# A two-layer mixer-and-expert network: the second layer's modulation vectors computed in pieces inside the first layer's expert loop, and the first block written out without its layer loop

## The chip, the cores and the metric

The kernel runs on one core of one Trainium2 chip. The metric is the device time of one launch in microseconds. The kernel before took 3701.41 us, median of three runs (3700.87 to 3701.83). All arithmetic is float32. Where full precision in a matrix product is wanted, each operand is split into an upper part, rounded to the fp32r type, and the remainder, and three products of the parts are added.

## The reference, cut to what matters

Two blocks follow each other, both two layers deep, on 256 tokens of width 1024. Only the first block is touched.

```python
cond = silu(c)                                   # c is (1, 1024): one vector for all tokens
for l in range(2):
    mod = cond @ ada_w[l] + ada_b[l]             # (1, 6144): six vectors of 1024
    sh1, sc1, g1, sh2, sc2, g2 = split(mod, 6)
    h = rms_norm(x, norm1_g[l]) * (1.0 + sc1) + sh1
    proj = h @ w_in[l]                           # then an SSD mixer, MoBA and sliding-window attention
    x = x + g1 * (concat(y_ssd, y_moba, y_swa) @ w_out[l])
    h = rms_norm(x, norm2_g[l]) * (1.0 + sc2) + sh2
    x = x + g2 * peer_ffn(h, ...)                # 8 heads x 16 of 16384 one-neuron experts
x = rms_norm(x, final_g)
# second block, unchanged: feed-forward, hybrid mixer, memory attention, feed-forward, twice
```

The modulation `mod` depends on `c` and the weights alone, not on `x`, in both layers. `ada_w[l]` is 1024 x 6144 floats, 24 MB. `peer_ffn` is computed densely: all 16384 experts are applied to all tokens, and a sparse matrix of gates picks the chosen ones.

## The kernel before, in words

Each engine has a program of its own; they meet at semaphores. The first block stands in a loop over the two layers (`Fori(0, DEPTH)`) on every engine. A layer has four stages.

1. The modulation stage. SyncE loads `ada_w[l]` in twelve tiles of 2 MB into the four slots of `weights` (L537). Of each tile's eight chunks of 128 rows VectorE multiplies and sums six (L1556, L1559), TensorE takes two (L763), adds the bias (L768) and sums VectorE's part over the partitions with a matrix of ones (L770), and ScalarE copies the row, which then stands on all partitions, to `mod` (L1147). After the fourth tile VectorE also normalizes `x` and `mem` (L1463, L1528, L1551). The end is `modulated` (L1534, L1538), which writes `h`, and TensorE transposes `mem` and `h` (L641).
2. The mixers, from the product with `w_in` (L718, L725, L685, L691) to the one with `w_out`, and then the queries and keys of the experts.
3. The choice of the experts on VectorE, beside the first layer of the experts' products.
4. The expert loops. The expert weights come in 256 parts of 1 MB for each layer of the network (here called steps; `expert_order` numbers them 0 to 127 per layer of the network). SyncE loads a part into one of four raw buffers. ScalarE makes its upper part (L1164), VectorE the lower (L1495; GpSimd, L622, for the first 22), TensorE multiplies: a step of the experts' first layer is L685 and L691 (`first_layer`), a step of the second is L923 (`second_layer`). TensorE goes through steps 0 to 19, then 20 to 35 with two groups of gates after each (L902; VectorE makes their one-hot tiles, L1825 and L1826), then 36 to 39; from step 40 on 12 rounds of two first-layer and two second-layer steps, and at last, in steps 88 to 127, second-layer steps alone. After each second-layer step VectorE waits for its end, gates the hidden values of one later step (L1842, L1843, L1845), and then makes a lower part two steps ahead. TensorE starts its accumulator banks with four products with zeros (L894) ahead of step 20, and closes them with L944. VectorE then multiplies by `g2` (L1870) and adds to `x` (L1874).

In this lace of rounds the order of every engine is fixed by the code; nothing is planned at run time. SyncE's queue carries all weight parts, the gates written to DRAM and read back (`scr<-gates`, 1 MB for every eight steps of the second layer), in the order of the code; ScalarE's queue carries the small parameter rows. Buffers on loan in stage 4: `mod` from column 2048 on and `rowp` hold activations of the experts (`gact`), so that `mod` holds only its first two vectors and the last one during the loops.

At the layer's end the loop branches back on all engines, and the modulation stage of the next layer begins. Its weights can be loaded as soon as the last expert parts have left the slots. Behind the second layer stands no modulation stage, but the final norm: there ScalarE takes the sum of squares (L1136) and a root (L1142), and VectorE a reciprocal (L1881) and one scaling (L1883).

## Time and profile before

| | |
|---|---|
| three runs | 3700.87 to 3701.83 us, median 3701.41 |
| the profiled execution | 3700.87 us, span 3699.1 us |
| TensorE busy | 3409.8 us (92%), mean granted clock 0.956 |
| VectorE, ScalarE, GpSimd busy | 2390.0, 1468.9, 229.0 us |
| first block, layer 0 | modulation 0 to about 89 us, experts' rounds and tail to 1099 us |
| first block, layer 1 | modulation 1099 to 1186 us, end at 2192 us |
| second block | 2192 to 3699 us |

The span runs from the first to the last instruction, and 1.8 us lie around it. A stage in which TensorE is busy throughout, with no wait recorded, is one whose length is TensorE's work; anything that another engine does there costs nothing as long as it is in time. A stage in which TensorE waits is one in which a chain through other engines sets the length.

### The profile page before, as it was taken

The numbers are of one execution on the slowest core, as the hardware profiler recorded it, in microseconds if no ns is written. First come the engines' busy times: TensorE is split into PE (matmuls) and PEld (weight loads), VectorE is DVE, ScalarE is ACT, GpSimd is POOL, SyncE is SP. The second block draws the span as 40 slices with busy tenths as digits, with TensorE's granted clock in tenths as the row PEclk, the third lists the DMA queues.
The fourth block names the chain that finished last, engine by engine and source line by source line (L and its number), as shares of the span: only waits on it lengthen the run. The fifth ranks groups of instructions, "written<-read, shape, count | busy, mean of one in ns | idle before, by whom it ended". The sixth has DMA issues, their size and how long they took to land.

```text
span 3699.1 us, 58720 instructions
## 1 busy us (share of the span) xinstructions
PE 3409.8 (92%) x22220; PEld 3087.8 (83%) x22220; DVE 2390.0 (65%) x4104; ACT 1468.9 (40%) x1545; POOL 229.0 (6%) x48
## 2 busy tenths in 40 slices
PE   6879999999997989999999989996989899978898
PEld 2879899998873879899998879896889798867897
DVE  6757996556768658996557765464545455546454
ACT  1434454333321434454343333444443343444433
POOL 0005600000000007500000000000000000000000
PEclk9989999999998989999999999997999999979999
DMA  9414467666767324466666765542335455423353
GB/s 367 171 69 160 157 222 251 207 211 225 245 215 316 137 103 161 163 223 239 213 214 228 246 233 191 182 171 80 138 140 184 168 179 195 158 102 123 142 183 137
DMA packets 154052, 688.78 MB, mean 186 GB/s; under 512 B 10339, under 2 KB 76771, under 8 KB 78947
## 3 DMA queue, kind: packets, MB, share of 16 engines
q1 hardware_dynamic: 149264, 663.79, 50.4%
q10 hardware_dynamic: 4564, 22.21, 1.6%
q8 instruction: 116, 1.90, 0.2%
q14 instruction: 108, 0.88, 0.1%
HBM read 649.26 MB, written 36.70 MB: 185 GB/s over the span
## 4 chain that ended last, share of the span: by engine, by line
PE 81%; DVE 10%; ACT 3%; issue 2%; DVEq 1%; DMA 1%; PEld 1%; ACTq 0%; PEldq 0%
PE ps L685 25%; PE ps L923 19%; PE ps L691 13%; PE ps L718 9%; PE ps L725 4%; PE ps L902 3%; DMA work<-in_mem 1%; ACT work L1156 1%; PE ps L763 1%; PE ps L657 1%; DVE position_hot L1802 1%; DVE position_hot L1805 1%; DVE scr L1767 1%; DVE scr L1760 1%; PE ps L770 1%
## 5 line engine op out<-in xcount | busy, mean ns | idle before, releaser
L1164 ACT ACTIVATE weights_upper<-weights 128x2048 fp32r<-128x2048 f32 x520 | 996.1, 1917 | 1694.4 <-PE ps L685 950.3
L1495 DVE TENSOR_TENSOR weights_lower<-weights,weights_upper 128x2048 fp32r<-128x2048 f32 x476 | 1090.3, 2291 | 749.1 <-ACT weights_upper L1164 748.3
L685 PE MATMUL ps<-hT_upper,weights_upper 128*128 128x256 f32 x4416 | 626.1, 284 | 3.5 <-ACT hT_upper L1326 3.5
L685 PE MATMUL ps<-hT_lower,weights_upper 128*128 128x256 f32 x4416 | 625.0, 284 | 0.2
L691 PE MATMUL ps<-hT_upper,weights_lower 128*128 128x256 f32 x4416 | 575.3, 283 | 4.1 <-POOL weights_lower L622 4.1
L685 PEld LDWEIGHTS ps<-hT_upper,weights_upper 128*128 128x128 f32 x4416 | 571.9, 192 | 7.1 <-ACT hT_upper L1326 6.7
L685 PEld LDWEIGHTS ps<-hT_lower,weights_upper 128*128 128x128 f32 x4416 | 571.1, 192 | 4.6 <-issue 1.0
L691 PEld LDWEIGHTS ps<-hT_upper,weights_lower 128*128 128x128 f32 x4416 | 549.7, 192 | 5.0 <-POOL weights_lower L622 5.0
L622 POOL TENSOR_TENSOR weights_lower<-weights,weights_upper 128x2048 fp32r<-128x2048 f32 x44 | 228.8, 5214 | 1299.3 <-ACT weights_upper L1164 1299.3
L923 PE MATMUL ps<-weights_upper,hidden_lower 128*128 128x512 f32 x1024 | 253.5, 390 | 0.0
L923 PE MATMUL ps<-weights_upper,hidden_upper 128*128 128x512 f32 x1024 | 252.9, 389 | 0.0
L923 PE MATMUL ps<-weights_lower,hidden_upper 128*128 128x512 f32 x1024 | 252.9, 389 | 0.0
L923 PEld LDWEIGHTS ps<-weights_lower,hidden_upper 128*128 128x128 f32 x1024 | 192.2, 188 | 39.9
L923 PEld LDWEIGHTS ps<-weights_upper,hidden_upper 128*128 128x128 f32 x1024 | 192.2, 188 | 39.9
L923 PEld LDWEIGHTS ps<-weights_upper,hidden_lower 128*128 128x128 f32 x1024 | 190.8, 188 | 38.5
L1826 DVE TENSOR_SCALAR scr<-cst,scr 128x128 f32<-128x128 f32 x512 | 187.7, 367 | 0.0
L1825 DVE TENSOR_SCALAR scr<-cst,scr 128x128 f32<-128x128 f32 x512 | 160.2, 313 | 0.2
L1842 DVE TENSOR_TENSOR hidden_upper<-work,scr 128x512 fp32r<-128x512 f32 x80 | 55.4, 693 | 119.3 <-PE ps L923 119.3
L902 PE MATMUL ps<-scr 128*128 128x128 f32 x1024 | 121.4, 277 | 0.0
L902 PEld LDWEIGHTS ps<-scr 128*128 128x128 f32 x1024 | 119.1, 191 | 0.0
L657 PE MATMUL ps<-diag,x_res 128*128 128x128 f32 x256 | 43.9, 351 | 59.6 <-DVE diag L1906 59.6
L718 PE MATMUL ps<-weights_upper,hT_lower 128*128 128x512 f32 (+2 forms) x352 | 91.6, 383 | 5.2 <-DVE hT_lower L1508 5.2
(311 smaller groups left out, 3478.7 us busy)
## 6 DMA issues: line engine op xcount, KB each, us to landing
weights<-in_parts SPq DMA_DIRECT2D x264, 1024.0 KB, 4.8
weights<-in_experts SPq DMA_DIRECT2D x256, 1024.0 KB, 4.8
weights<-in_ada_w SPq DMA_DIRECT2D x24, 2048.0 KB, 11.3
scr<-gates SPq DMA_DIRECT2D x32, 1024.0 KB, 8.1
gates<-h SPq DMA_DIRECT2D x16, 1024.0 KB, 4.8
gates<-work SPq DMA_DIRECT2D x16, 1024.0 KB, 4.8
mod<-in_row ACTq DMA_DIRECT2D x3, 1536.0 KB, 6.2
rowp<-in_row ACTq DMA_DIRECT2D x2, 1550.0 KB, 19.6
```

Source lines behind the costliest of these rows:

```text
L622: g.tensor_tensor(lower[:, p_.r % SPLIT, :], raw[:, p_.r, :], upper[:, p_.r % SPLIT, :].bitcast(F32), ALU.subtract).then_inc(lower_ready, 1)
L657: m = mm(k.bank(name, i)[:, (2 * e + t) * P:(2 * e + t + 1) * P], x[:, t, c * P:(c + 1) * P], diag[:, t, :], start=True, stop=True, skip_g ...
L685: m = mm(bank[:, e * T:(e + 1) * T], up[:, c, e * P:(e + 1) * P], s_[:, c, :], start=(e == 0 and n == 0 and c == 0), stop=False, skip_grou ...
L691: m = mm(bank[:, e * T:(e + 1) * T], lo[:, c, e * P:(e + 1) * P], src[0][:, c, :], start=False, stop=(c == KC - 1), skip_group_check=True)
L718: m = mm(k.bank(name, fill + t)[:, 0:cols], s_[:, c, t * P:(t + 1) * P], up[:, c - 4 * i, 0:cols], start=(n == 0 and c == 0), stop=False, ...
L725: m = mm(k.bank(name, fill + t)[:, 0:cols], src[0][:, c, t * P:(t + 1) * P], lo[:, c - 4 * i, 0:cols], start=False, stop=(c == chunks - 1) ...
L902: m = mm(k.bank("G", j)[:, t * P:(t + 1) * P], hotA[:, i_buf, 4 * j + t, :], hotB[:, i_buf, 4 * j + t, :], start=True, stop=True, skip_gro ...
L923: m = mm(k.bank("acc", 2 * t_ + dh), src[:, u, c, t_ * P:(t_ + 1) * P], w[:, c, dh * NBLK:(dh + 1) * NBLK], start=False, stop=False, skip_ ...
L1164: f(upper[:, p_.r % SPLIT, :], raw[:, p_.r, :], ACT.Copy).then_inc(upper_ready, 1)
L1495: v.tensor_tensor(lower[:, s, :], raw[:, p_.r, :], upper[:, s, :].bitcast(F32), ALU.subtract)\
L1825: v.tensor_scalar(hotA[:, i % 2, j, :], iota, ET[:, 0, t:t + 1], None, ALU.is_equal)
L1826: m = v.tensor_scalar(hotB[:, i % 2, j, :], iota, ET[:, 1, t:t + 1], ET[:, 2, t:t + 1], ALU.is_equal, ALU.mult)
```

## The change

Layer 0's modulation stage stays. For layer 1 the stage is gone. In its place:

- The weights `ada_w[1]` come as 96 pieces of 128 x 512 floats, 256 KB each (`ada_s`), eight for each of twelve stretches of 512 columns. SyncE loads them between the expert parts of layer 0 into four buffers in `work` (`load_ada`).
- VectorE adds each piece, times its value of `cond`, to an accumulator in `scr` (`ada_piece`, L1986). `ada_sub_step` gives the step: six pieces in each of the 12 rounds (two in the first step, two in the second, one in the third, one in the fourth), and one in each of the steps 88 to 111.
- Two steps after a stretch's last piece TensorE sums it over the partitions with one column of ones (`ada_rows`, L946), a product of one row by 512 columns; ScalarE copies that row out in two halves (L1369); SyncE writes them to DRAM (`keep_row`, 1 KB each). Twelve times each.
- ScalarE's queue reads the vectors back onto all partitions (`mod_back`), in three transfers at steps 88 and 112 and after the layer, and loads layer 1's `rowp` at step 118. At step 122 VectorE makes `(1 + sc1) * norm1_g` (L2017).
- At the layer's end ScalarE takes squares and roots as for the final norm, and VectorE makes `h` with `scaled_and_shifted` (a reciprocal, L1688, L1691). The first two parts of `w_in[1]` have their upper and lower parts made in steps 126 and 127.
- The first block is written out on all engines, TensorE's rounds too; the waits there compare with constants. The products with zeros moved from ahead of step 20 to after step 39, on both layers.

```diff
+def ada_sub_step(s):
+    turn, i = divmod(s, 6)
+    if turn < TURNS - AHEAD:
+        return 2 * AHEAD + 4 * turn + (0, 0, 1, 1, 2, 3)[i]
+    return 2 * AHEAD + 4 * (TURNS - AHEAD) + s - 6 * (TURNS - AHEAD)
...
@@ SyncE @@
+                def load_ada(s):
+                    tile = s // KC
+                    if s % KC == 0:
+                        if tile:
+                            sp.wait_ge(S("ada_used"), s - 7)
+                        else:
+                            sp.wait_ge(S("bias_zero"), 1)
+                        sp.dma_start(ada_bias_row[0:1, :], a["ada_b"][1:2, tile * NBLK:(tile + 1) * NBLK])\
+                            .then_inc(S("ada_bias_in"), 16)
+                    if s >= 4:
+                        sp.wait_ge(S("ada_used"), s - 3)
+                    sp.dma_start(ada_sub(s), a["ada_s"][s]).then_inc(ada_landed[s % 4], 16)
+                def keep_row(tile):
+                    sp.wait_ge(*k.emptied("row", 0, tile))
+                    for b in range(2):
+                        c = tile * NBLK + b * (NBLK // 2)
+                        sp.dma_start(ada_dram[0:1, c:c + NBLK // 2], ada_row[b]).then_inc(ada_kept[b], 16)
                 for n, (layer, t, u) in enumerate(expert_order()):
                     e = expert_part(l, 0, n)
                     sp.wait_ge(*e.raw_free())
+                    sp.dma_start(raw[:, e.r, :], a["experts"][l, n]).then_inc(raw_landed[e.r], 16)
+                    if l + 1 < DEPTH:
+                        for s in range(ADA_SUBS):
+                            if ada_sub_step(s) + 4 == n:
+                                load_ada(s)
...
+                            if ada_sub_step(KC * tile + KC - 1) + 10 == n:
+                                keep_row(tile)
...
@@ TensorE @@
-            with pe.Fori(0, DEPTH) as l:
+            for l in range(DEPTH):
...
-                for i in range(12):
+                for i in range(0 if l else 12):
...
+                def ada_rows(n):
+                    for tile in range(ADA_TILES if l + 1 < DEPTH else 0):
+                        if ada_sub_step(KC * tile + KC - 1) + 2 == n:
+                            pe.wait_ge(*k.free("row", 0, tile))
+                            pe.wait_ge(S("ada_used"), KC * tile + KC)
+                            mm(k.bank("row")[0:1, :], ones[:, 0:1], ada_acc[tile % 2], start=True, stop=True,
+                               skip_group_check=True).then_inc(k.fill_sem("row"), 1)
...
-                with pe.Fori(0, TURNS - AHEAD) as it:
-                    for u in range(2):
-                        first_layer(it, 2 * AHEAD + u, it + AHEAD, u)
-                    for u in range(2):
-                        second_layer(it, 2 * AHEAD + 2 + u, it, u)
...
+                for n in range(2 * AHEAD, EXPERTS):
+                    layer, t, u = order[n]
+                    (first_layer, second_layer)[layer](n, t, u)
+                    ada_rows(n)
...
@@ ScalarE, in the loop over the steps n @@
+                    elif l + 1 < DEPTH:
+                        upper_part(part(firsts[l + 1], 0, "win", n + SPLIT - EXPERTS))
+                    if l + 1 < DEPTH:
+                        for tile in range(ADA_TILES):
+                            if ada_sub_step(KC * tile + KC - 1) + 3 == n:
+                                ada_take(tile)
+                        if n == 2 * AHEAD + 4 * (TURNS - AHEAD):
+                            mod_back(0, 2)
+                        if n == 112:
+                            act.wait_ge(S("gated"), 2 * (AHEAD + 3))
+                            mod_back(2, 5)
+                        if n == 118:
+                            act.wait_ge(S("gated"), 2 * (AHEAD + 6))
+                            row1_in(1)
...
+                    for t in range(TT):
+                        act.wait_ge(S("x_peer"), l * TT + (t + 1))
+                        square_sum(x[:, t, :], h[:, t, :], t)
+                        deviation(t, t, EPS1_COL)
...
@@ VectorE @@
+                def ada_piece(s):
+                    tile, i = divmod(s, KC)
+                    acc = ada_acc[tile % 2]
+                    if i == 0:
+                        if tile >= 2:
+                            v.wait_ge(*k.filled("row", 0, tile - 2))
+                        v.wait_ge(S("ada_bias_in"), 16 * tile + 16)
+                        v.sem_inc(S("held"), 1)
+                    v.wait_ge(ada_landed[s % 4], 16 * (s // 4) + 16)
+                    v.drain()
+                    v.scalar_tensor_tensor(out=acc, in0=ada_sub(s), scalar=cT[:, i:i + 1],
+                                           in1=acc if i else ada_bias_row, op0=ALU.mult, op1=ALU.add)\
+                        .then_inc(S("ada_used"), 1)
...
                     if n + SPLIT < EXPERTS:
                         lower_part(expert_part(l, 0, n + SPLIT))
+                    elif l + 1 < DEPTH:
+                        lower_part(part(firsts[l + 1], 0, "win", n + SPLIT - EXPERTS))
...
+                    scaled_and_shifted(mod[:, D:2 * D], mod[:, 0:D], TT, "h1")
```

On VectorE, in a round before, the two first-layer steps and the first of the two second-layer steps; L1495 makes a lower part, L1842 to L1845 gate hidden values, and the rows between compute what a wait compares with:

```order
L1495 TENSOR_TENSOR weights_lower<-weights,weights_upper 128x2048
L1493 REGISTER_ALU
L1495 TENSOR_TENSOR weights_lower<-weights,weights_upper 128x2048
L1855 REGISTER_ALU
L1834 REGISTER_ALU
L1842 TENSOR_TENSOR hidden_upper<-rowp,scr 128x512
L1843 TENSOR_TENSOR rowp<-rowp,scr 128x512
L1845 TENSOR_TENSOR hidden_lower<-rowp,hidden_upper 128x512
L1493 ISA
L1495 TENSOR_TENSOR weights_lower<-weights,weights_upper 128x2048
```

And in the changed kernel, layer 0, the same steps, from behind the first lower part; L1613 is the lower part, L1969 to L1972 the gating, L1986 the pieces:

```order
L1986 SCALAR_TENSOR_TENSOR scr<-work,stats,scr 128x512 x2
L1613 TENSOR_TENSOR weights_lower<-weights,weights_upper 128x2048
L1986 SCALAR_TENSOR_TENSOR scr<-work,stats,scr 128x512 x2
L1969 TENSOR_TENSOR hidden_upper<-mod,scr 128x512
L1970 TENSOR_TENSOR mod<-mod,scr 128x512
L1972 TENSOR_TENSOR hidden_lower<-mod,hidden_upper 128x512
L1613 TENSOR_TENSOR weights_lower<-weights,weights_upper 128x2048
L1986 SCALAR_TENSOR_TENSOR scr<-work,stats,scr 128x512
```

A piece always stands behind the lower part of its step, so it delays the gating of the next step and not the lower part of its own.

On TensorE, at the seam of the two layers before: the last second-layer step, the closing of the accumulators, and then, by way of the branch to the loop's head at L754, the modulation stage:

```order
L923 MATMUL ps<-weights_upper,hidden_upper 128x512 x8
L932 REGISTER_ALU
L923 MATMUL ps<-weights_lower,hidden_upper 128x512 x8
L940 REGISTER_ALU
L940 COMPARE_AND_BRANCH
L944 MATMUL ps<-cst 128x2 x4
L754 REGISTER_ALU
L754 COMPARE_AND_BRANCH
```

In the changed kernel the same place; L699 transposes `h` of layer 1, L776 is the product with the first part of `w_in`:

```order
L989 MATMUL ps<-weights_upper,hidden_upper 128x512 x8
L989 MATMUL ps<-weights_lower,hidden_upper 128x512 x8
L1006 MATMUL ps<-cst 128x2 x4
L699 MATMUL ps<-cst,h 128x128 x16
L776 MATMUL ps<-weights_upper,hT_upper 128x512 x4
L776 MATMUL ps<-weights_upper,hT_lower 128x512 x4
```

All of the modulation stage and the transposes of `mem` are gone from between them, and no branch is left.

On VectorE at the same seam, the changed kernel; L2028 and L2032 add the experts' output to `x`, L1626 makes the lower part of the transposed `h`:

```order
L1972 TENSOR_TENSOR hidden_lower<-work,hidden_upper 128x512
L1613 TENSOR_TENSOR weights_lower<-weights,weights_upper 128x2048 x3
L2028 TENSOR_TENSOR scr<-ps,mod 128x512 x2
L2032 TENSOR_TENSOR x_res<-x_res,scr 128x1024
L2028 TENSOR_TENSOR scr<-ps,mod 128x512 x2
L2032 TENSOR_TENSOR x_res<-x_res,scr 128x1024
L1686 RECIPROCAL stats<-stats 128x1
L1688 SCALAR_TENSOR_TENSOR h<-x_res,stats,mod 128x1024
L1691 TENSOR_TENSOR h<-h,mod 128x1024
```

Of the three lower parts two are new there, those of `w_in`; before they stood behind the modulation stage.

## Rows read from the trace of the kernel before

**Rows 1.** Busy time by stage: us, PE, PEld, DVE, ACT, POOL busy (instructions), clock, DMA share, GB/s.

```profile
871.00:1100.00 229.00, 229.00 (x1016) 189.75 (x1014) 170.01 (x162) 77.53 (x42) 0.00 (x0) 1.00 0.66 222
1100.00:1186.00 86.00, 59.46 (x124) 20.01 (x124) 68.79 (x100) 14.82 (x21) 0.00 (x0) 0.84 0.86 351
```

**Rows 2.** Timeline, layer 0 to layer 1: start us, us, engine, line, instruction, [idle before].

```profile
1099.50 0.95 PE L944 MATMUL ps<-cst 128*128 128x2 f32 x8
1099.82 1.29 DVE L1870 TENSOR_TENSOR scr<-ps,mod 128x512 f32<-128x512 f32 x2 [6.73 <-PE ps L944]
...
1110.90 0.08 DVE L1523 MEMSET work<- 128x24 f32 x1 [5.96 <-issue]
...
1183.66 2.36 DVE L1538 TENSOR_TENSOR h<-h,mod 128x1024 f32<-128x1024 f32 x2
...
1187.86 1.83 PE L718 MATMUL ps<-weights_upper,hT_upper 128*128 128x512 f32 x4
...
1192.28 1.82 PE L718 MATMUL ps<-weights_upper,hT_lower 128*128 128x512 f32 x4 [2.59 <-DVE hT_lower L1508]
...
1198.59 1.07 PE L718 MATMUL ps<-weights_upper,hT_upper 128*128 128x512 f32 x4
```

**Rows 3.** Timeline, layer 1 to the second block.

```profile
2191.69 0.95 PE L944 MATMUL ps<-cst 128*128 128x2 f32 x8
...
2197.15 0.29 ACT L1142 ACTIVATE stats<-stats 128x1 f32<-128x1 f32 x1
...
2197.79 1.28 DVE L1883 SCALAR_TENSOR_TENSOR x_res<-x_res,stats,scr 128x1024 f32<-128x1024 f32 x1
```

**Rows 4.** Timeline of TensorE in the rounds of the experts.

```profile
624.37 2.00 PE L923 MATMUL ps<-weights_upper,hidden_lower 128*128 128x512 f32 x8
...
635.28 1.12 PE L685 MATMUL ps<-hT_lower,weights_upper 128*128 128x256 f32 x8
...
646.79 2.00 PE L923 MATMUL ps<-weights_upper,hidden_lower 128*128 128x512 f32 x8
```

**Rows 5.** Timeline of VectorE in one of these rounds.

```profile
635.48 0.69 DVE L1842 TENSOR_TENSOR hidden_upper<-mod,scr 128x512 fp32r<-128x512 f32 x1 [0.73 <-PE ps L923]
...
637.46 2.29 DVE L1495 TENSOR_TENSOR weights_lower<-weights,weights_upper 128x2048 fp32r<-128x2048 f32 x1
```

**Rows 6.** Timeline, modulation stage: five sums, a product, and two weight loads.

```profile
1160.33 4.05 DVE L1559 SCALAR_TENSOR_TENSOR mod<-weights,stats,mod 128x512 f32<-128x512 f32 x5
...
1161.79 1.13 PE L770 MATMUL ps<-mod,cst 128*128 128x512 f32 x2
...
1163.79 0.19 PEld L763 LDWEIGHTS ps<-weights,stats 128*128 128x128 f32 x1 [0.24 <-issue]
...
1164.22 0.19 PEld L763 LDWEIGHTS ps<-weights,stats 128*128 128x128 f32 x1 [0.24 <-issue]
```

**Rows 7.** Timeline where the gate groups begin and end.

```profile
434.12 5.79 PE L894 MATMUL ps<-cst 128*128 128x512 f32 x8 [0.36 <-DVE scr L1475]
...
464.88 2.29 DVE L1495 TENSOR_TENSOR weights_lower<-weights,weights_upper 128x2048 fp32r<-128x2048 f32 x1
474.33 2.29 DVE L1495 TENSOR_TENSOR weights_lower<-weights,weights_upper 128x2048 fp32r<-128x2048 f32 x1
...
576.82 3.79 PE L902 MATMUL ps<-scr 128*128 128x128 f32 x32
...
586.20 3.79 PE L902 MATMUL ps<-scr 128*128 128x128 f32 x32
```

**Rows 8.** DMA issues in 871 to 1090 us: KB each, median us to landing.

```profile
weights<-in_experts SPq DMA_DIRECT2D x37, 1024.0 KB, 4.9
scr<-gates SPq DMA_DIRECT2D x9, 1024.0 KB, 8.2
```

**Rows 9.** DMA issues in 1100 to 1180 us.

```profile
rowp<-in_row ACTq DMA_DIRECT2D x1, 1550.0 KB, 13.8
colp<-in_col ACTq DMA_DIRECT2D x1, 148.0 KB, 15.3
```

315 lines of the change are left out of this document (188 added, 127 removed).

## The prediction

> **What bounds the kernel now.** I read the table of stages first, to see where TensorE has no idle time, then the list of TensorE's waits, then the order of time at the two seams of the first block. In 871 to 1100 us, layer 0's last expert steps, TensorE is busy for all 229 us at the full clock, while VectorE works 170 of them and the DMA engines are busy for 0.66 of the time [rows 1]. TensorE alone sets the length there: what another engine gets on top is free as long as it stays in time, and every product added on TensorE is paid. The modulation stage of layer 1 behind it is the opposite. In its 86 us TensorE has 59 us of work, much of it at half speed (the granted clock is 0.84 on average), and VectorE is the busier one with 69 us [rows 1]. The stage's weights come at 351 GB/s [rows 1]. The change takes this stage away, and puts its sums under a stage in which VectorE has room.
>
> **The seam.** I measure from the products that close the accumulators to the start of the second part of `w_in`: 1198.59 - 1099.50 = 99.1 us before [rows 2]. After the change nothing of the modulation is left there, and the nearest measured thing is the seam between layer 1 and the second block, where the same square sums and roots are made [rows 3]. Step by step from the closing products:
>
> - Two lower parts of `w_in` now stand ahead of VectorE's addition to `x`. The last one waits for TensorE's last product, so it starts where L1870 started, 0.32 us after the closing products began [rows 2], and takes 2.29 us [rows 5]: 2.3 us of delay.
> - From the closing products to the end of the first token half's root: 2197.44 - 2191.69 = 5.75 us [rows 3].
> - Then VectorE: a reciprocal (0.35 us to the start of the next), a scaling of 1.28 us [rows 3], an addition of 1.18 us (2.36 for two) [rows 2], some 0.1 us between: 2.9 us for each half, and the halves follow each other. 5.8 us.
> - From the last `h` to TensorE's first product with `w_in`: 1187.86 - 1186.02 = 1.8 us (1186.02 is 1183.66 + 2.36) [rows 2]. This holds the transposes and ScalarE's first copy.
> - The first four products take 1.83 us, the rest of the first part 1198.59 - 1192.28 = 6.3 us [rows 2]. The wait of 2.59 us between them [rows 2] was for VectorE, busy with the same two lower parts that are now made before; it goes. What is late next is the chain of ScalarE's copy and VectorE's subtraction, which fits in the 1.83 us.
>
> Sum: 2.3 + 5.75 + 5.8 + 1.8 + 1.8 + 6.3 = 23.8 us, where there were 99.1. **The seam gives 75.3 us.** The bounds are 70 (VectorE's and ScalarE's small waits a half longer) and 79 us (no delay by the lower parts, shorter halves).
>
> Part of these 99.1 us was the loop's own: VectorE's first instruction of layer 1 comes at 1110.90 with 5.96 us of idle that nothing recorded released [rows 2], behind its branch back. The Trainium skill (Runtime: NRT & Kernel Launch, section Instruction fetch mechanics) says that a taken branch out of the current pages waits for a fetch of code. The row agrees; by that rule the straight code has no such pause, and were it there still, the seam would give 6 us less.
>
> **Products added on TensorE.** Twelve sums over partitions, one each of 512 columns in plain float32. Such a product is two passes in the trace, and in a run of them the passes start 1164.22 - 1163.79 = 0.43 us apart [rows 6], 0.86 us each; one alone shows 1.13 us to its modelled end [rows 6]. Between the other products it costs its passes, with the next one's load beside it. 12 x 0.86 = 10.3, at most 12 x 1.13 = 13.6. I take 10.7 us. Nothing hides them, since TensorE has no idle time there.
>
> **Pieces added on VectorE.** 96 sums of 128 x 512. Five in a row with the drains took 4.05 us [rows 6], 0.81 us each, 78 us in all. A round takes TensorE 646.79 - 624.37 = 22.42 us, and a second-layer step half of 635.28 - 624.37, 5.45 us [rows 4]. In such a step VectorE starts the gating, 1.98 us later the lower part, and is done after 2.29 more [rows 5]: 4.27, with a piece 5.08 us of 5.45. In a first-layer step a lower part and two pieces are 3.9 us of (22.42 - 10.91) / 2 = 5.76. So every step closes in itself, and a gated value, needed one step after the end that VectorE waits for, has 5.45 - 0.6 - 1.98 = 2.9 us in hand. The pieces are hidden: 0 us. If the cover is gone, the waiting order is gating, lower part, TensorE. The far ends are 0 and 78 us (all on the path). The nearest row, VectorE in its rounds, speaks for 0, and I keep +4 for the 24 tight steps.
>
> **Transfers.** Six pieces a round are 1.6 MB. At 0.66 busy [rows 1] the DMA engines work 14.8 us of a round; at the 351 GB/s and 0.86 of the modulation stage [rows 1] the pieces take 1.6 / 0.351 x 0.86 = 3.9 us more, 0.83 of the round. An expert part lands in 4.9 us, a block of gates in 8.2 [rows 8], and a part is asked for about three steps ahead of its use, 15 us. The pieces are asked for two steps ahead, 11 us. Small transfers in the crowded stage landed in up to 15.3 us, though behind large ones [rows 9]. I take 0 us, with +8 as the other end. `rowp` has four steps and 5 us, about 27 us, to land before VectorE waits for it at step 122, with gating queued behind it; it took 13.8 [rows 9].
>
> The Trainium skill (DMA: Bandwidth & Descriptors, section Bandwidth) speaks against the cut: its rule is transfers of 1 MiB or more for three quarters of the peak, and these are 256 KB. Were their cost twice mine by that rule, an estimate, the DMA engines would be busy for 22.6 of 22.4 us, and the rounds would just become theirs.
>
> **Zeros moved.** The four products with zeros stood right behind a pause of TensorE and took 5.79 us to their modelled end [rows 7], part of it at 1.2 GHz, since at the other level four products are 4 x 0.86 = 3.4 us. That is what they take after step 39. Step 20 now meets the low clock and loses the 2.4 us of difference. But the gate groups are tied to VectorE too: its lower parts there come 9.45 us apart, with no idle, and TensorE's groups 9.38 us apart [rows 7]. So TensorE gains little by starting early and then pays the 3.4 us: I take +1 us a layer, 2 us, between -4 and +7.
>
> **Constants in the waits.** The register arithmetic ahead of waits goes on both layers, and so do the branches of the rounds. The rounds follow without a gap (10.91 + 2 x 5.76 is the 22.42 seen) [rows 4], so there is nothing to win in them. In the mixers I take -2 us in all, between 0 and -12.
>
> **Sum.** -75.3 + 10.7 + 0 + 0 + 2 - 2 = -64.6 us. The profiled execution took 3699.1 + 1.8 = 3700.9 us, 0.5 below the median of the runs. 3700.9 - 64.6 = 3636.3, and with the median's 0.5: **3637 us**. The bounds above give 3618 to 3662.
>
> **Rivals.**
>
> *VectorE comes late.* A piece costs more than its 0.81 us once its reading stands beside incoming transfers, or the waits between add up. At 1.3 us a second-layer step needs 5.6 us of 5.45, which costs 24 x 0.15 = 4 us in the tail; at 2.2 us, nearly three times the measured one, TensorE waits 1.0 us in each, which costs 25. For it speaks the thin margin of 0.37 us a step, against it that these sums ran at 0.81 us under the kernel's highest DMA rate [rows 1, 6]. Time: 3637 + 25 = 3662.
>
> *The transfers bind the rounds.* With the pieces at twice the price, plus gates, each of the 12 rounds and the 24 tail steps waits about 1 us: 36 us, 3673. Against it is the idle 0.34 of the DMA engines.
>
> *TensorE starves for code* (the slower side). The rounds ran from a short body held in a loop; now each step's 96 or so instructions and more are streamed, next to weights at 0.8 of the DMA engines. The place is every step of both layers, 256 in all, and it decides from 64.6 / 256 = 0.25 us a step. At 0.4 us it would be 102 us: 3739. Against it: VectorE's and ScalarE's code for these steps was straight already, and TensorE's code in the mixers is straight and runs without gaps.
>
> *More is saved.* If the pauses of the small stages were mostly register arithmetic and the mixers give 12 us: 3625.
>
> *Nothing happens*, the stage being replaced by another wait of the same length, say for the vectors read back from DRAM: these are asked for at steps 88 and 112, 40 and 16 steps of 5.45 us ahead of use. I give it 1 in 100.
>
> **How the numbers follow.** Forecast 0.72; VectorE late 0.10; transfers 0.05; more saved 0.09; code 0.03; nothing 0.01. The range is 3620 to 3665: it holds the forecast's bounds and most of the rivals on both sides. A measurement tells 0.2% (7 us) from no change. Faster 0.95, same 0.02, slower 0.03, as only the last two cases leave that side.
>
> **What would show it.** Between the closing products and the second part of `w_in` about 24 us; the twelve products one by one at 0.86 us distance added; no wait of TensorE in steps 40 to 127, with a round of layer 0 at 22.42 or 23.3 us; VectorE's pieces at 0.75 us busy; DMA busy about 0.8; layer 1 from there on as long as before, within 5 us. Waits of TensorE for lower parts, hidden parts or `weights_upper` in layer 0's rounds would make it wrong, as would idle time of TensorE between its own instructions.

## The result, and the profile after

The changed kernel took 3641.87 us, median of four runs (3641.30 to 3643.28), beside 3701.62 us (3700.87 to 3702.02) for the kernel before on the same chip: a ratio of 0.984, 95% interval 0.9829 to 0.9852. That is 59.8 us less, where 64.6 were forecast, and inside the range. The profiled execution has a span of 3640.6 us against 3699.1, with the same mean granted clock of 0.956.

First the stages. TensorE's first instruction of each marks its start, and the columns are microseconds.

| stage | before | after | difference | forecast |
|---|---|---|---|---|
| start to the experts chosen, layer 0 | 432.23 | 432.24 | 0 | 0 |
| gate groups to step 42, layer 0 | 192.14 | 194.27 | +2.13 | +1 |
| rounds and tail, layer 0 | 475.13 | 489.09 | +13.96 | +10.7 |
| the seam | 99.09 | 22.79 | -76.30 | -75.3 |
| mixers and choice, layer 1 | 325.75 | 324.97 | -0.78 | -2 |
| gate groups to step 42, layer 1 | 192.22 | 193.98 | +1.76 | +1 |
| rounds and tail, layer 1 | 475.13 | 475.13 | 0 | 0 |
| second block | 1507.4 | 1508.1 | +0.7 | 0 |

The sum is -58.5 us, the difference of the spans (3640.6 - 3699.1). The forecast's large term held; the row products are 3.3 us above it, and the gate stages, the mixers and the second block 1.9, 1.2 and 0.7 us.

Busy time by stage in the changed kernel, in the columns of [rows 1]; the second stretch is the seam:

```profile
871.00:1100.00 229.00, 229.00 (x1044) 187.72 (x1044) 191.84 (x190) 82.30 (x53) 0.00 (x0) 1.00 0.82 282
1116.00:1138.00 22.00, 11.13 (x44) 9.29 (x45) 14.89 (x18) 8.81 (x14) 0.00 (x0) 0.61 0.23 89
```

In the same 229 us as in [rows 1] VectorE works 191.8 us instead of 170.0 and the DMA engines are busy for 0.82 instead of 0.66, but TensorE has still no idle time and the full clock. The seam has 22 us where there were 99 us.

Most of that window lies in the tail, with one piece a step. The rounds, with six pieces each, before and then after:

```profile
655.00:871.00 216.00, 216.00 (x1406) 198.51 (x1405) 124.96 (x96) 84.23 (x58) 0.00 (x0) 1.00 0.62 212
655.00:885.00 230.00, 230.00 (x1444) 203.33 (x1443) 172.83 (x158) 89.75 (x75) 0.00 (x0) 1.00 0.78 271
```

The timeline of the seam, which answers to [rows 2]:

```profile
1115.60 0.95 PE L1006 MATMUL ps<-cst 128*128 128x2 f32 x8
1115.98 2.29 DVE L1613 TENSOR_TENSOR weights_lower<-weights,weights_upper 128x2048 fp32r<-128x2048 f32 x1 [3.15 <-ACT weights_upper L1226]
1118.19 1.28 DVE L2028 TENSOR_TENSOR scr<-ps,mod 128x512 f32<-128x512 f32 x2
...
1123.33 0.29 ACT L1204 ACTIVATE stats<-stats 128x1 f32<-128x1 f32 x1
...
1123.89 1.28 DVE L1688 SCALAR_TENSOR_TENSOR h<-x_res,stats,mod 128x1024 f32<-128x1024 f32 x1
...
1126.62 1.94 PE L699 MATMUL ps<-cst,h 128*128 128x128 f32 x8 [10.08 <-DVE h L1691]
...
1127.98 1.23 DVE L1691 TENSOR_TENSOR h<-h,mod 128x1024 f32<-128x1024 f32 x1
...
1130.95 2.06 PE L776 MATMUL ps<-weights_upper,hT_upper 128*128 128x512 f32 x4
...
1138.39 1.07 PE L776 MATMUL ps<-weights_upper,hT_upper 128*128 128x512 f32 x4
```

The reader finds each step of the forecast's chain. The lower part of `w_in` puts VectorE's first multiplication off to 1118.19, 2.59 us behind the closing products (forecast 2.3 behind the 0.32 us of before). The first root ends 8.02 us behind them (8.05 forecast), the last `h` 13.61 (13.85), TensorE's first product with `w_in` follows 1.74 us later (1.8), and the first part takes 7.44 us (8.1). TensorE's pause of 10.08 us waits for `h`. The pause at the loop's branch is gone. One link came out in number only: the profile puts the start of that lower part down to ScalarE's upper part, which is made from 1114.03 to 1115.95, and not to TensorE's last product, as the forecast had it. TensorE's last product ends at 1115.76, within 0.2 us of it, so the 2.3 us were met partly by luck.

In the rounds, TensorE around one of the twelve row products (L946), and PEld's rows for the loads there:

```profile
652.59 1.97 PE L989 MATMUL ps<-weights_lower,hidden_upper 128*128 128x512 f32 x8
654.49 1.02 PE L946 MATMUL ps<-scr,cst 128*1 128x512 f32 x2
655.44 2.11 PE L989 MATMUL ps<-weights_upper,hidden_lower 128*128 128x512 f32 x8
```
```profile
654.49 0.09 PEld L946 LDWEIGHTS ps<-scr,cst 128*1 128x1 f32 x2 [0.35 <-issue]
655.44 1.69 PEld L989 LDWEIGHTS ps<-weights_upper,hidden_lower 128*128 128x128 f32 x8 [0.86 <-ACT weights_upper L1226]
```

A group of eight products takes 1.815 us from start to start. From 652.59 to the group behind the next one, at 657.39, there are 4.80 us with the row product in between, so it costs 4.80 - 2 x 1.815 = 1.17 us, and twelve cost 14.0: the whole growth of the rounds. The steps bear this out. In the tail, second-layer steps start 5.44 us apart in both kernels, with a piece on VectorE or without; only at a row product are two distances 6.48 and 5.57 us, which is 1.17 us more for the pair. PEld shows no load for 0.86 us while the two passes run, and the next load begins at 655.44, in the moment in which its own product does. Elsewhere loads run ahead of the products: those for the group at 652.59 begin at 652.37.

VectorE in a step of the tail, with a piece:

```profile
987.24 0.76 DVE L1986 SCALAR_TENSOR_TENSOR scr<-work,stats,scr 128x512 f32<-128x512 f32 x1
988.33 0.69 DVE L1969 TENSOR_TENSOR hidden_upper<-mod,scr 128x512 fp32r<-128x512 f32 x1 [0.33 <-PE ps L989]
...
990.30 2.29 DVE L1613 TENSOR_TENSOR weights_lower<-weights,weights_upper 128x2048 fp32r<-128x2048 f32 x1
992.68 0.75 DVE L1986 SCALAR_TENSOR_TENSOR scr<-work,stats,scr 128x512 f32<-128x512 f32 x1
```

A piece is 0.75 us busy as forecast, and 5.44 us on (992.68 - 987.24) the next one comes. In each step VectorE idles for 0.33 us, waiting for TensorE, where 0.37 was forecast. TensorE has no wait recorded between 626 and 1116 us.

The DMA issues in 655 to 1090 us (columns as in [rows 8]):

```profile
weights<-in_experts SPq DMA_DIRECT2D x76, 1024.0 KB, 4.9
work<-in_ada_s SPq DMA_DIRECT2D x84, 256.0 KB, 5.3
scr<-gates SPq DMA_DIRECT2D x14, 1024.0 KB, 8.4
```

An expert part lands in 4.9 us as before [rows 8]. A piece takes 5.3 us, and is asked for 8.6 to 14.6 us ahead of its sum (forecast 11).

### The profile page after: what moved, and what is told of

Read it like the earlier page. It is cut to its first block, busy times and chain, and to the rows that moved or that the text cites. A ratio compares the mean times of both kernels' runs of the same rounds, so it can differ in the third digit from the quotient of the medians.

```text
span 3640.6 us, 55813 instructions
## 1 busy us (share of the span) xinstructions
PE 3371.6 (93%) x22132; PEld 3074.8 (84%) x22132; DVE 2403.5 (66%) x4114; ACT 1475.0 (41%) x1559; POOL 229.4 (6%) x48
## 4 chain that ended last, share of the span: by engine, by line
PE 81%; DVE 11%; ACT 3%; issue 2%; DMA 1%; DVEq 1%; PEld 1%; ACTq 0%; PEldq 0%
PE ps L743 25%; PE ps L989 19%; PE ps L749 13%; PE ps L776 9%; PE ps L783 4%; PE ps L967 3%; ACT work L1218 1%; DMA work<-in_mem 1%; DVE position_hot L1929 1%; PE ps L715 1%; DVE position_hot L1932 1%; DVE scr L1894 1%; DVE scr L1887 1%; DVE work L1888 1%; PE ps L1040 1%
## 5 line engine op out<-in xcount | busy, mean ns | idle before, releaser
L1613 DVE TENSOR_TENSOR weights_lower<-weights,weights_upper 128x2048 fp32r<-128x2048 f32 x476 | 1096.2, 2304 | 727.9 <-ACT weights_upper L1226 726.8
L1953 DVE TENSOR_SCALAR scr<-cst,scr 128x128 f32<-128x128 f32 x512 | 226.3, 544 | 0.0
L1952 DVE TENSOR_SCALAR scr<-cst,scr 128x128 f32<-128x128 f32 x512 | 217.7, 491 | 0.2
L1969 DVE TENSOR_TENSOR hidden_upper<-work,scr 128x512 fp32r<-128x512 f32 x80 | 55.4, 692 | 97.1 <-PE ps L989 97.0
L699 PE MATMUL ps<-cst,h 128*128 128x128 f32 x128 | 29.5, 419 | 78.5 <-DVE h L2318 30.5
```

The source lines that it names most:

```text
L1613: v.tensor_tensor(lower[:, s, :], raw[:, p_.r, :], upper[:, s, :].bitcast(F32), ALU.subtract)\
L1952: v.tensor_scalar(hotA[:, i % 2, j, :], iota, ET[:, 0, t:t + 1], None, ALU.is_equal)
L1953: m = v.tensor_scalar(hotB[:, i % 2, j, :], iota, ET[:, 1, t:t + 1], ET[:, 2, t:t + 1], ALU.is_equal, ALU.mult)
```

## The experiments

Of the twelve kernels below most change one thing in the kernel before or after, and one (changed_again) is the changed kernel itself. Each ran with the kernel before on the same chip; a sum of stages is from the profiled execution. The stages, in microseconds, with "choice" for the start to the experts chosen and "second" for the second block:

| kernel | choice | gates 0 | rounds 0 | seam | mixers 1 | gates 1 | rounds 1 | second |
|---|---|---|---|---|---|---|---|---|
| before | 432.2 | 192.14 | 475.13 | 99.09 | 325.8 | 192.22 | 475.13 | 1507.4 |
| straight | 432.6 | 193.58 | 475.13 | 97.90 | 325.7 | 193.58 | 475.13 | 1502.5 |
| after | 432.2 | 194.27 | 489.09 | 22.79 | 325.0 | 193.98 | 475.13 | 1508.1 |
| changed_again | 432.5 | 194.40 | 489.08 | 22.87 | 325.0 | 194.08 | 475.13 | 1508.2 |
| rows_short | 435.5 | 194.42 | 479.29 | 21.82 | 323.6 | 194.10 | 475.12 | 1508.3 |
| rows_full | 432.9 | 194.40 | 485.76 | 22.86 | 325.0 | 194.10 | 475.13 | 1508.2 |
| pieces_twice | 436.3 | 194.41 | 492.90 | 21.83 | 323.5 | 194.12 | 475.13 | 1505.0 |
| copies | 436.6 | 194.39 | 489.08 | 21.96 | 321.9 | 194.11 | 475.13 | 1506.9 |
| zeros_back | 432.7 | 194.64 | 489.08 | 22.70 | 325.0 | 191.58 | 475.13 | 1507.1 |
| lower_late | 432.5 | 194.24 | 489.09 | 20.08 | 330.1 | 193.92 | 475.13 | 1506.0 |
| together | 433.6 | 194.88 | 485.75 | 19.86 | 330.0 | 192.96 | 475.13 | 1506.9 |
| two_edits | 432.3 | 194.64 | 485.75 | 22.64 | 325.0 | 191.56 | 475.12 | 1507.1 |
| filled | 431.8 | 194.24 | 489.08 | 24.18 | 323.5 | 193.94 | 475.13 | 1501.9 |
| late_filled | 433.0 | 194.23 | 489.08 | 23.19 | 325.0 | 193.93 | 475.13 | 1501.9 |

The rounds repeat to 0.01 us, so an effect there is read off directly. The other stages wander by some microseconds, and where a trace was looked at, by where the granted clock rises. Each kernel has one trace, while the runs of one kernel differ by up to 11.6 us (two_edits, 3634.17 to 3645.80), so a stage's length is that of the execution with the trace.

**straight.** The kernel before with the layer loop of the first block written out, and nothing of the modulation moved.

```diff
-            with pe.Fori(0, DEPTH) as l:        # and so on SyncE, GpSimd, ScalarE, VectorE
+            for l in range(DEPTH):
```

> The kernel before with only its outer loop over the two layers of the first block written out; the modulation stage of layer 1, TensorE's inner loops and the place of the zeros stay. Theory (the change wins by removing the stage, little by the straight code): the pause of about 6 us at VectorE's branch goes, but the stage's weights still come as before, so 4 to 8 us less than 3701.6, about 3695, and the mixers of layer 1 shorter by under 1 us. Rival (the straight code itself is a good part of the gain): 15 us or more less, 3686 or below.

Measured 3698.54 us (3695.54 to 3699.87), ratio 0.9991, interval 0.9982 to 1.0. That is 2.5 us less than the kernel before on that chip, under the 4 to 8 that I expected. So the written-out code by itself is at most a few microseconds of the gain. The pause at the branch, 5.96 us in [rows 2], is gone in VectorE's timeline:

```profile
1105.54 1.23 DVE L1874 TENSOR_TENSOR x_res<-x_res,scr 128x1024 f32<-128x1024 f32 x1
1106.99 0.49 DVE L1556 TENSOR_SCALAR mod<-weights,stats 128x512 f32<-128x512 f32 x1 [0.22 <-issue]
```

Yet the seam is only 1.2 us shorter. The chain that ended last there now holds 30.09 us of the load of `mem`, from 1108.06 on: what VectorE gained at the branch it gives back waiting for loads. The table shows more: the whole 3 us of span came from the second block (4.9 us less, without a changed instruction). In the first block straight code cost 1.4 us in each gate stage. There TensorE's gate groups (L902; the two behind a step are 32 products, merged into one row) are a little slower:

```profile
455.51 3.85 PE L902 MATMUL ps<-scr 128*128 128x128 f32 x32
```

against 3.79 us in [rows 7], with these pairs of groups 9.44 us apart (455.51 - 446.07) where they were 9.38. In the changed kernel they are 9.50 apart:

```profile
575.27 3.92 PE L967 MATMUL ps<-scr 128*128 128x128 f32 x32
584.77 3.92 PE L967 MATMUL ps<-scr 128*128 128x128 f32 x32
```

Over 15 distances that is 1.8 us a layer, nearly the whole growth of the gate stages. Neither TensorE nor VectorE has as much as 0.3 us of idle time in 455 to 585 us, before or after. Why the groups are slower stays open.

**rows_short and rows_full**, on the price of a row product. In the first the sum is cut from 512 to 8 columns (504 columns of each vector's stretch are left out of it), in the second it is made with all 128 columns of the ones.

```diff
-mm(k.bank("row")[0:1, :], ones[:, 0:1], ada_acc[tile % 2], start=True, stop=True,
+mm(k.bank("row")[0:1, 0:8], ones[:, 0:1], ada_acc[tile % 2][:, 0:8], start=True, stop=True,   # rows_short
+mm(k.bank("row"), ones, ada_acc[tile % 2], start=True, stop=True,                             # rows_full
```

> The changed kernel with the twelve sums over partitions cut from 512 to 8 columns; the other 504 columns of each are left out. Theory (a sum costs its two passes of 0.43 us and 0.3 us of change-over around them): 12 x 0.84 = 10 us less, 3631.8, and 0.3 us each remain. Rival (the 1.17 us of each are a wait for another engine, VectorE's last piece or ScalarE's copy): the same time, 3641.9.

Measured 3633.46 us (3632.44 to 3634.73), ratio 0.9816, interval 0.9802 to 0.9829. The rounds are 479.29 us, 4.2 more than before: 0.35 us for each product of almost no columns. So of the 1.17 us, 0.82 go with the 504 columns that are left out, and 0.35 don't.

> The changed kernel, with each of the twelve sums over the partitions made with all 128 columns of the ones, so that the product is 128x512 like its neighbours and the first partition of its result is what is copied on. Theory A (the 0.35 us beside the two passes is the change to a one-column load, which a load of full width does not have): 0.86 to 0.95 each instead of 1.17, 3639.0 us. Theory B (the 0.35 us is the change between bf16 and float32 products, or the load of the ones that cannot go ahead): 1.17 or a little more each, 3641.9 to 3644 us.

Measured 3639.28 us (3638.21 to 3642.09), ratio 0.9836, interval 0.982 to 0.9853; the rounds are 485.76 us. That is (485.76 - 475.13) / 12 = 0.89 us each, and theory A holds. The change to plain float32, in theory B, is still there (the neighbours multiply fp32r parts, not bf16 ones), and the 0.3 us are gone. TensorE around one of them:

```profile
653.42 1.98 PE L989 MATMUL ps<-weights_lower,hidden_upper 128*128 128x512 f32 x8
655.23 1.02 PE L946 MATMUL ps<-scr,cst 128*128 128x512 f32 x2
655.69 2.42 PE L989 MATMUL ps<-weights_upper,hidden_lower 128*128 128x512 f32 x8
657.95 1.98 PE L989 MATMUL ps<-weights_upper,hidden_upper 128*128 128x512 f32 x8
```

From 653.42 to 657.95 there are 4.53 us, 4.80 with the one-column form. The loads of the same product, on PEld:

```profile
655.01 0.41 PEld L946 LDWEIGHTS ps<-scr,cst 128*128 128x128 f32 x2
655.66 0.19 PEld L989 LDWEIGHTS ps<-weights_upper,hidden_lower 128*128 128x128 f32 x1 [0.24 <-ACT weights_upper L1226]
```

The load for the sum begins 0.22 us ahead of its product, and PEld is idle for 0.24 us and not for 0.86 before the next load. Making 128 rows of output where one is wanted is cheaper by 0.28 us. What is shown is that the width of the load makes the difference; why a one-column load isn't taken ahead stays open.

The trace of before had a nearer row than the one that the forecast used. In its modulation stage a product stands beside one whose stationary operand has another shape, one partition of 128 columns:

```profile
1156.39 1.12 PE L768 MATMUL ps<-work,cst 1*128 1x512 f32 x2
1157.44 1.12 PE L770 MATMUL ps<-mod,cst 128*128 128x512 f32 x2
```

L768 costs 1157.44 - 1156.39 = 1.05 us at a granted clock of 1.00, and not 0.86. So a change of the load's shape had a price there already, though no run shows that it is the same one.

**pieces_twice.** Whether VectorE's sums are hidden, and by what margin.

```diff
+                    v.scalar_tensor_tensor(out=acc, in0=ada_sub(s), scalar=cT[:, i:i + 1],
+                                           in1=acc if i else ada_bias_row, op0=ALU.mult, op1=ALU.add)
+                    v.drain()
                     v.scalar_tensor_tensor(out=acc, in0=ada_sub(s), scalar=cT[:, i:i + 1],
```

> The changed kernel, but each of the 96 pieces is multiplied and added twice on VectorE (so the vectors' values are not the reference's); transfers and row products as in the changed kernel. A second sum is 0.75 us as the first, so a step with a piece has 0.75 us more on VectorE, a round of four steps with eight pieces 6.0 us less what stood idle. Theory (the sums are hidden, but with a thin margin): VectorE now does some 5.5 to 5.9 us in a step that TensorE makes in 5.6 us, so the cover gives out and the twelve rounds of layer 0 come out 1 to 2 us longer each: 3655 to 3665 us against 3641.9. Rival (VectorE still has room, or its time never counts): 3641.9 us again. Rival (VectorE set the rounds already in the changed kernel): all of 96 x 0.75 = 72 us is added, 3714 us.

Measured 3644.86 us (3644.28 to 3648.91), ratio 0.9854, interval 0.9837 to 0.987: 3 us more than the changed kernel, and far from the 13 to 20 I expected. Part of this was an error of mine: a round has six pieces, not eight, so its added work is 4.5 us and still fits. VectorE in the tail:

```profile
984.42 0.75 DVE L1986 SCALAR_TENSOR_TENSOR scr<-work,stats,scr 128x512 f32<-128x512 f32 x1
985.25 0.75 DVE L1989 SCALAR_TENSOR_TENSOR scr<-work,stats,scr 128x512 f32<-128x512 f32 x1
...
987.89 2.29 DVE L1613 TENSOR_TENSOR weights_lower<-weights,weights_upper 128x2048 fp32r<-128x2048 f32 x1
990.26 0.75 DVE L1986 SCALAR_TENSOR_TENSOR scr<-work,stats,scr 128x512 f32<-128x512 f32 x1
```

The period is 990.26 - 984.42 = 5.84 us, with no idle time: here VectorE is the slower engine, by 0.4 us a step. Over 24 steps it falls back by 9.4 us, and the rounds and tail grow by 3.8 us (492.90 - 489.09). TensorE's steps stay as they were for the first 14 of the tail, and then go at VectorE's 5.84 us until the pieces end. So the first 5.6 us of the lag show nowhere: VectorE had that much in hand. 96 more sums, 72 us of VectorE's time, cost 3.8 us. So one set of them costs nothing, as forecast.

**copies.** Whether the transfers are near their bound.

```diff
                     sp.dma_start(ada_sub(s), a["ada_s"][s]).then_inc(ada_landed[s % 4], 16)
+                    sp.dma_start(spare_dram[s], a["ada_s"][s]).then_inc(S("spare"), 16)
```

> The changed kernel, with a copy of each piece (256 KB, from DRAM to a spare place in DRAM) issued right behind its load on the same queue: 96 more transfers, so the pieces' traffic is doubled, and nothing waits for the copies before the kernel's end. Theory (the transfers do not bind the rounds of layer 0): 3641.9 us again, within 3. Rival (the transfers are just under the bound, so what is added shows): the pieces' own share of the engines, about 3 us in a round, comes once more on twelve rounds, 36 us: 3678 us, with VectorE or TensorE waiting for weights in the rounds.

Measured 3641.73 us (3641.61 to 3642.48), ratio 0.9843, interval 0.9826 to 0.9859: nothing lost. The stretch of 655 to 1090 us, columns as in [rows 1]:

```profile
655.00:1090.00 435.00, 435.00 (x2334) 368.63 (x2333) 345.64 (x333) 162.81 (x120) 0.00 (x0) 1.00 0.92 332
```

The DMA engines are busy for 0.92 at 332 GB/s, and the rounds are 489.08 us as without the copies. So the forecast's "0 us" had at least this much room.

**zeros_back.** The products with zeros ahead of step 20 again.

```diff
+                for i in range(4):       # ahead of step 20, and taken out behind step 39
+                    pe.wait_ge(*k.free("acc", i))
+                    mm(k.bank("acc", i), zeros, cst[:, 0:NBLK], start=True, stop=False, skip_group_check=True)
```

> The changed kernel with the four products with zeros back ahead of step 20, on both layers. Theory (the gate groups are set by VectorE's one-hot tiles, so the zeros' place ahead of them was free): step 42 of both layers comes 1.8 to 2.1 us earlier after the experts' choice, 3.9 us in all, 3638.0. Rival (the move costs nothing, the 3.9 us come from the straight rounds): 3641.9.

Measured 3640.77 us (3639.69 to 3648.54), ratio 0.9846, interval 0.9832 to 0.9859. In layer 1 the gate stage falls by 2.4 us to 191.58; in layer 0 it doesn't fall at all (194.64). The products with zeros and what follows them, in layer 0 and in layer 1 of this kernel:

```profile
434.61 6.02 PE L962 MATMUL ps<-cst 128*128 128x512 f32 x8 [0.36 <-DVE scr L1593]
440.06 1.52 PE L743 MATMUL ps<-hT_lower,weights_upper 128*128 128x256 f32 x8
...
1465.53 3.70 PE L962 MATMUL ps<-cst 128*128 128x512 f32 x8 [0.56 <-DVE scr L1593]
1468.66 1.52 PE L743 MATMUL ps<-hT_lower,weights_upper 128*128 128x256 f32 x8
```

They take 5.45 us in layer 0, at a mean granted clock of 0.60, and 3.13 us in layer 1, at 1.00. That difference of 2.3 us makes most of what sets the two layers' stages apart (194.64 and 191.58): it comes from the clock at that place, and not from the place in the order. In together the same products of layer 1 take 4.15 us, and the stage is 192.96. In both layers the groups stay 9.50 us apart, so the slower groups aren't the move's doing.

**lower_late.** The second lower part of `w_in` taken from ahead of the addition to `x` to behind the modulated `h`.

```diff
-                    elif l + 1 < DEPTH:
+                    elif l + 1 < DEPTH and n + 1 < EXPERTS:
                         lower_part(part(firsts[l + 1], 0, "win", n + SPLIT - EXPERTS))
...
                     scaled_and_shifted(mod[:, D:2 * D], mod[:, 0:D], TT, "h1")
+                    lower_part(win_late)
```

> The changed kernel with the lower part of w_in's second part made behind the modulated h instead of ahead of VectorE's addition to x. Theory (it delays the whole seam): the addition starts 2.2 us earlier, the seam is 20.6 instead of 22.8 us, 3639.7. Rival (the lower part then delays the subtraction that TensorE waits for, behind the transposes): 3641.9 or a little more, the delay moved to TensorE's first product with hT_lower.

Measured 3642.17 us (3635.14 to 3642.89), ratio 0.9835, interval 0.9821 to 0.9848. Four of the five runs lie at 3641.46 or above and one at 3635.14; the trace is of the slowest, 3642.89. In it the seam gave the 2.7 us, and the mixers behind it took 5.1 us more: here is TensorE's pause at the seam, and after it the mixers' rows, of this kernel.

```profile
1115.80 0.95 PE L1006 MATMUL ps<-cst 128*128 128x2 f32 x8
1124.56 1.94 PE L699 MATMUL ps<-cst,h 128*128 128x128 f32 x8 [7.81 <-DVE h L1691]
```
```profile
1135.90:1466.00 330.10, 299.43 (x2209) 289.80 (x2207) 235.73 (x615) 136.22 (x154) 110.15 (x22) 0.92 0.38 134
```

The same 2209 products are busy for 299.4 us, at a granted clock of 0.92. The run of 3635.14 has no trace, so whether its mixers were longer isn't known.

**together.** zeros_back, lower_late and rows_full in one.

> The changed kernel with three edits in one: the products with zeros in the gate phase's step 20 again, the second row product of w_in's lower part behind the modulated h, and the sums with all 128 columns of the ones. Theory (what each did by itself adds up where the clock allows): 1.9 us from the zeros in layer 1's gate phase, 2.7 us at the seam, 0 to 2.6 us from the sums: 3635 to 3637 us. Rival (the seam's gain is taken back by the mixers of layer 1 at the clock's hand, as when it was made alone): 3637.5 to 3640 us.

Measured 3639.49 us (3637.58 to 3640.8), ratio 0.9834, interval 0.9818 to 0.9851. The sums and the seam gave what they gave alone (485.75 and 19.86 us), and the mixers took 330.0 us again: the rival holds in the trace and in the median. The gate stage of layer 1 gave 1.0 of the 2.4 us.

**changed_again, two_edits, late_filled, filled**, on one chip, to find what made the mixers longer. two_edits is zeros_back with rows_full. The other two have an addition at the seam, which is made again by what follows it:

```diff
                         v.wait_ge(*k.filled("acc", i))
+                        if l == 0 and i == 0:
+                            v.memset(h[:, :, :], 0.0)
+                            v.drain()
+                            v.memset(h[:, 0, 0:384], 0.0)
```

> The changed kernel itself, as the measure for the three others of this chip. 3641.9 us, as before, within 1.5.

Measured 3645.53 us (3642.02 to 3648.59), ratio 0.9853, interval 0.9837 to 0.9868. The stages are those of the changed kernel. But the median is 3.7 us above that of the changed kernel on the first chip, more than the 1.5 that I allowed: the run with the trace took 3643.0, and two others about 3648 that no trace explains.

> The changed kernel with the sums made with all 128 columns of the ones, and the products with zeros in step 20 again; the lower part at the seam stays where it is. Theory (both add up, and nothing at the seam gives the clock another course): 2.6 and 1.1 us less, 3638.2 us, and the mixers of layer 1 at 325 us and not 330. Rival (whatever is taken away comes back in the mixers): 3639.5 to 3641.9 us.

Measured 3636.40 us (3634.17 to 3645.8), ratio 0.9832, interval 0.9819 to 0.9846, span 3634.0. The mixers are at 325.0 us and the two gains are there (rounds -3.3, gate stage of layer 1 -2.5): by the stages the theory holds, though the second gain hangs on the clock at the zeros. It is the lowest median of those that leave nothing out, though its interval overlaps that of changed_again.

> The changed kernel with w_in's second lower part behind the modulated h, as in the run of that edit alone, and with 2.4 us of clearing h on VectorE at the place where the lower part was (h is written anew right behind it). So TensorE's pause at the seam is as long as in the changed kernel again, some 10 us, but the lower part stands late. Theory (the length of TensorE's pause gave the clock its other course): seam 22.5 us, mixers of layer 1 325 us, 3642 us. Rival (the place of the lower part in the order makes the mixers longer): seam 22.5, mixers 330, 3647 us.

Measured 3637.30 us (3636.99 to 3639.55), ratio 0.983, interval 0.9817 to 0.9844. The seam is 23.2 us with a pause of 10.45 us, and the mixers are back at 325.0 us with the lower part in its late place. Changed_again and late_filled in the mixers:

```profile
1138.80:1463.80 325.00, 291.94 (x2209) 282.73 (x2207) 235.67 (x615) 136.20 (x154) 110.12 (x22) 0.95 0.39 137
```
```profile
1139.50:1464.50 325.00, 291.94 (x2209) 282.73 (x2207) 235.91 (x615) 136.23 (x154) 110.14 (x22) 0.95 0.39 137
```

TensorE's busy time is the same to the hundredth, 291.94 us. So the late place of the lower part doesn't make the mixers longer by itself. Late_filled differs from lower_late only in the clearing of `h`, which makes the pause longer; the mixers start 3.6 us later, and the clock takes the other course. Whether the pause's length or the time of the start decides isn't shown, and each side rests on one or two traces. The total is 4.7 us below the theory's 3642: that came from the second block (1501.9 us), as in the next kernel.

> The changed kernel with the same 2.4 us of clearing h on VectorE ahead of the addition at the seam, and nothing else: TensorE's pause is 12.5 us instead of 10.1. Theory (a longer pause does the mixers no harm, and may leave them up to 3 us shorter): seam 25.2 us, mixers 322 to 325 us, 3641.5 to 3644.3 us. Rival (the mixers' length has nothing to do with the pause): exactly 2.4 us more than the changed kernel, 3644.3.

Measured 3637.09 us (3635.64 to 3638.8), ratio 0.9829, interval 0.9815 to 0.9842. With 2.4 us of useless work added, the span is 7.4 us shorter than that of changed_again. The mixers give 1.5 us (the theory's side), but 6.2 us come from the second block, which neither of my two theories had. All five runs of filled lie below all four of changed_again. In the second block, TensorE in changed_again, and then in filled:

```profile
2539.74 3.19 PE L699 MATMUL ps<-cst,h 128*128 128x128 f32 x14
2542.58 2.06 PE L776 MATMUL ps<-weights_upper,hT_upper 128*128 128x512 f32 x4
```
```profile
2538.68 2.64 PE L699 MATMUL ps<-cst,h 128*128 128x128 f32 x13
2541.07 1.22 PE L776 MATMUL ps<-weights_upper,hT_upper 128*128 128x512 f32 x4
```

The same four products take 2.06 us at the low level (1.2 GHz) or 1.22 us mostly at the high one. The full clock comes back a few microseconds earlier there, and again at such a place later: in the 20 us from 3279 us in changed_again the granted clock is 0.66, in those from 3278 us in filled 0.83. Which event far ahead decides it stays open, and so does whether two_edits with the addition would be lower still, since it wasn't run.

## Why the prediction was right, and where a size was off

**The seam: right, -76.3 for -75.3.** Every link of the chain fell within 0.7 us of its forecast, the largest miss being the first part of `w_in`. The delay by the lower part was right with the wrong releaser, ScalarE's upper part for TensorE's last product. Rows from a seam of the same form [rows 3] were a good measure of one that did not yet exist. The Trainium skill (Runtime: NRT & Kernel Launch, section Instruction fetch mechanics) lets a taken branch wait for code when its target isn't in the current pages; the 5.96 us at the branch [rows 2] vanish in straight, as the rule has it. By themselves they were worth 1.2 us, as loads took up the rest.

**Products added on TensorE: right in kind, too small, +14.0 for +10.7.** The step "between the other products it costs its passes, with the next one's load beside it" failed. The passes are 0.86 us as said [rows 6]. But beside them came 0.3 us of the change to a one-column load and back, which rows_short shows as the remainder of 0.35 us and rows_full shows gone, at 0.89 us each. My source row had full-width loads, and gave the price of a full-width product to 0.03 us; the row of L768, at 1.05 us beside a load of another shape, would have warned me. This term makes 3.3 of the 6.1 us by which the spans' difference (-58.5) fell short of -64.6; the gate stages, the mixers and the second block make the rest (1.9, 1.2 and 0.7), less the 1.0 that the seam gave above its forecast. By the medians the shortfall is 4.9 us.

**Pieces: right, 0.** The margin of 0.37 us a step was measured as 0.33, the tail's steps with a piece kept their 5.44 us, and pieces_twice showed that even minus 0.4 costs 3.8 us in all. The +4 kept for the tight steps wasn't needed, and the rival "VectorE comes late" falls.

**Transfers: right, 0.** I worked out 0.83 for a round from the 0.66 of a window that lies mostly in the tail. In the rounds it was 0.62 before and 0.78 after, and the added 0.16 is 3.6 us of a round where I had 3.9; the tail's 0.82 looks nearer to my figure than it is. The rule of the Trainium skill (DMA: Bandwidth & Descriptors, section Bandwidth) that asks for 1 MiB or more was weighed as the rival at twice the price. That would have shown as 1.0 busy and waits. This trace doesn't agree with it here: between loads of 1 MB the pieces of 256 KB raised the busy share of the rounds by 0.16 and the traffic by 59 GB/s (271 - 212), and with as many copies on top 332 GB/s flowed without a wait of TensorE. The price of that rival, 1 us in each of 36 places, also didn't follow from its own sum, 22.6 us of work in 22.4.

**Zeros moved and constants: small, both a little low.** The two gate stages are 3.9 us longer, 2 forecast, and what I had named for it, the zeros' 3.4 us at their new place, isn't what grew. The slower gate groups, 9.50 us apart for 9.38, make 1.8 us a layer, and zeros_back has them too with the zeros in their old place. The move by itself comes to some -0.4 us in layer 0 (194.27 for 194.64). In layer 1 it is +2.4, where in zeros_back the zeros met the full clock, which my "part of it at 1.2 GHz" took for fixed. In the mixers -0.8 us came of the -2. Stages there differ by more than that from kernel to kernel, so it isn't a measured effect.

**The slower rival** (TensorE starves for code) needed 0.25 us a step. Layer 1's rounds and tail, written out, took 475.13 us, as the loop did, and layer 0's steps without a row product are as long as before at 0.78 to 0.82 of the DMA engines: 0.00 us a step. The 0.12 us in each step with gate groups is the one place where straight code went with longer steps, and whether the code is the cause isn't shown.

The bounds of the terms add up to 3617 and 3664 us, not to the 3618 and 3662 of the forecast; the range of 3620 to 3665 leaves out 3 us at the lower end.

The result was forecast well because its two large terms lay in stages with one plain limit each: a chain that can be followed link by link, and an engine that has no idle time.

## What to carry to other kernels

Work that feeds a later stage and doesn't depend on the one now running can be hidden on an engine with room, but each instruction that it leaves on the bounding engine is paid in full: count them, and take their price from a row with the same neighbours and the same shape of load. A margin of 6% (0.33 of 5.45 us) on the covering engine is enough where buffers lie between, and it may even be overdrawn for some steps. Differences of up to 6 us in 3640 came from where the clock rises in stages that nothing touched, and runs of one kernel lay up to 11.6 us apart; a claim smaller than this needs the stage in which it was made, not the total.

## What the runs showed that I had not expected

- A float32 sum of 512 columns with a one-column stationary cost 1.17 us between full-width products, and the same sum with 128 equal columns 0.89 us.
- A shorter pause of TensorE (7.81 instead of 10.08 us) was followed by 5.1 us more in the mixers, in the one trace that each of two kernels has (lower_late and together, 7.81 us in both); with a pause of 10.45 us, and a later start, the 5.1 us were gone.
- 2.4 us of added useless work was followed by a second block of 1501.9 us in filled and late_filled alike, 6.2 us less than in changed_again and 4.1 less than in lower_late. In straight it was 1502.5 us.
- Groups of 32 small products ran at 3.79 us in the loop, 3.85 in straight, and 3.92 in the changed kernel.
- The same eight passes with zeros took 5.45 us in layer 0 and 3.13 in layer 1 of one execution, at granted clocks of 0.60 and 1.00.
